# HGRN2 and pooling step on one Trainium2 core: transposing the decayed keys on VectorE and through memory instead of on TensorE

## Chip, cores and metric

One of the eight cores of a Trainium2 chip (trn2) runs the whole step. The metric is the device time of one execution in microseconds (us). TensorE is PE in the profile, VectorE is DVE, ScalarE is ACT, GpSimd is POOL, and SyncE, which issues every DMA of this kernel, is SP.

## What is computed

One inference step of a single layer: a gated linear recurrence (HGRN2) with four heads of 128 x 128 state, beside a pooling branch, both gated and merged. 2048 prompt tokens and 8 x 4 sample tokens pass the same weights. Cut to what the change touches:

```python
z = rmsnorm(x) @ w_in                       # split into q, f, i, g_a, u, g_b, m_a, m_b
fgate = lb + (1 - lb) * sigmoid(f)
logf, kin = log(fgate), 1 - fgate
# in chunks of 32 tokens, b = cumsum(logf) inside the chunk, ref = b at its middle
scores = (q * exp(b - ref)) @ (kin * exp(ref - b)).T        # masked to s <= t
o = scores @ v + (q * exp(b)) @ S
S = exp(b_last) * S + (kin * exp(b_last - b)).T @ v
o = rmsnorm(o) * silu(g_a)
out = x + (sigmoid(m_a) * (o @ w_proj_a) + sigmoid(m_b) * y_pool) @ w_out
```

All is float32. A large product is done as three products of values that are split into a high and a low part (`hi*hi + lo*hi + hi*lo`).

## The kernel before

The 2080 tokens go in five tiles of T = 416 tokens (features on the partitions, tokens along the free axis); the last tile has 384 prompt tokens and the 32 sample tokens. Each tile has NU = 56 slots, one for each block of weights, 128 x 1024. Slots 0 to 15 are the four heads, four slots each in the order f, q, i, g; then come the pooling inputs `u` and gates `b` (16 to 23), the merge gates and the two projections (24 to 47), and `out` (48 to 55). A slot is 24 matmuls of 128 x 416 on PE (`three`, L484 to L486).

Every engine has its program written out by slot, in one order that never changes; engines meet at semaphores. Weights flow so: SP loads block s + 2 into `wraw` in its slot s, after DVE has made the low part of block s (L401, L402). ACT in slot s copies block s + 3 into `whi` once PE has finished slot s - 1 (L763, L823), and DVE makes `wlo` of it at the start of its own slot s (`split`, L992). So SP is in its slot s when DVE is in slot s - 3, and both follow PE.

The recurrence of head h:

- slot 4h + 4: DVE makes the gate (`gated`, L1024), the state updates of head h - 1 (`updates`, L1110; in the last tile after the sums, with four of its eight sample states), the running sum of `logf` (`sums`, L1032 and L1042), `queries` (q2 and e1 at L1049 and L1051, four small copies of decays into `fac` at L1055, a scan into `dec`, the decayed queries `q4` at L1062). ACT makes the exponentials e3, e1, e2, e4 (`decays`, L797 to L805). POOL multiplies `e2` and `e4` by the keys (L1486, L1488).
- slot 4h + 5: DVE's `decayed_keys` (L1092) makes `qr0`, `qr1` and `kj4`, the keys decayed to the end of each 128-token block.
- slot 4h + 7: PE transposes `kj4` (L576, three of 128 x 128) and the last 32 columns of `e4` (L577) into bank B7, and computes the scores (L516 to L521). ACT copies the transposes to `ktm` (L837, L841). DVE copies the masked scores (`scores`, L1077 to L1082).
- slot 4h + 8: PE multiplies `ktm` with the values `vtm` (L539).
- slot 4h + 9: PE makes the outputs (`outputs`, L625, and L635, which waits for three state updates of DVE in its slot 4h + 8).

The values go another way. DVE transposes them in blocks of 32 x 32 (`values`, L1001 to L1003), and SP sends them out to `v_blocks` in memory with four DMAs, one for each 32 partitions, in pieces of 128 bytes (`values_out`, L455, slot 4h + 7), and back with two DMAs (`values_in`, L466 and L467, slot 4h + 9). That is where blocks change place.

The normed output of tile t - 1 is made by DVE in slots 5 to 8 of tile t, two of its eight parts in each slot (`output`, L1335), right after `split`. SP stores all 1,664 KB of it in slot 11 (`y_store`, L471), after the last part is made. Two more DMAs of that size are the loads of `xin` (L406) and `xres` (L433).

Of the kernel before, what the change touches and what calls it, by code (L numbers as in the profile page):

```python
# [114 lines left out]
def step_kernel(nc, xT, w_all, consts, w_pool, s_in, buf_in, yT, sp_out, pp_out, ss_out, ps_out):  # L115
    with ExitStack() as ctx:
# [57 lines left out]
        og = [buf["og0"], buf["og1"]]  # L174
        vt, logf, bc, dd, dl = buf["vt"], buf["logf"], buf["b"], buf["d"], buf["dl"]
# [91 lines left out]

        v_mem = nc.dram_tensor("v_blocks", (T, P), F32, kind="Internal").ap()
# [31 lines left out]
        kj_made, dq_made, ktm_made = sem("kj_made"), sem("dq_made"), sem("ktm_made")  # L300
# [6 lines left out]
        smasks, so_done, so_made, split_k, split_v = (sem("smasks"), sem("so_done"), sem("so_made"), sem("split_k"),  # L307
# [57 lines left out]

        def win_value(t, last, g, level, sample=False):
            before = sum(range(1, g + 1)) * (2 if last else 1)
            return t * 10 + before + (2 * level + sample if last else level) + 1
# [8 lines left out]
        def _(sp):  # L377
# [13 lines left out]
            def tile(t, last):  # L391
                for s in range(NU):
                    for h in range(H):
                        if s == 4 * h + 7:
                            values_out(t, h)
                        if s == 4 * h + 9:
                            values_in(t, last, h)
                    n = s + RAW
# [20 lines left out]
                    if last and s in (13, 17, 21, 25):  # L419
                        h = (s - 13) // 4  # L420
# [28 lines left out]
            def values_out(t, h):  # L449
# [30 lines left out]
        def _(pe):  # L480
# [7 lines left out]
            def small(t, last, s):  # L488
                for h in range(H):
# [5 lines left out]
                    if s == base + 7:  # L495
# [3 lines left out]
                        if not h:  # L499
                            pe.wait_ge(ybm_made, t * G)  # L500
                        elif last:
                            pe.wait_ge(s_made, s_value(t, last, h - 1, NG + 3))
                        else:
                            pe.wait_ge(ktm_made, nth(t, H, h - 1))
                        transposes(B7, kj4[:].rearrange("p g j n -> p (g j n)"), tk_done, e4)


# [17 lines left out]
                    if s == base + 8:  # L525


                        pe.wait_ge(ktm_made, nth(t, H, h))
# [24 lines left out]
                if s in MIX_SLOT:  # L553
# [4 lines left out]
                    if g == 1:  # L558
                        pe.wait_ge(ktm_made, nth(t, H, H - 1))
                    if g < 2:  # L560
# [3 lines left out]
                    three((B6, B7)[g % 2][:, 0:T], (wph[:, g, :], wplo[:, g, :]),  # L564
# [8 lines left out]

            def transposes(bank, src, done, rest):
                for g in range(NG):
                    pe.transpose(bank[:, g * P:(g + 1) * P], src[:, g * P:(g + 1) * P], ident[:])  # L576
                pe.transpose(bank[0:SAMPLE, 3 * P:4 * P], rest[:, PT:T], ident[:]).then_inc(done, 1)  # L577
# [181 lines left out]
        def _(act):  # L759
# [59 lines left out]
            def tile(t, last):  # L819
                for s in range(NU):  # L820
# [6 lines left out]
                    for h in range(H):  # L827
# [6 lines left out]
                        if s == 4 * h + 7:  # L834
                            act.wait_ge(tk_done, nth(t, H, h))
                            rest = B7[0:SAMPLE, 3 * P:4 * P]
                            act.activation(ktm[:, 0:3, :], B7[:, 0:3 * P].rearrange("p (g v) -> p g v", v=P), ACT.Copy)  # L837
                            if last:
                                high_rows(ks, rest, 1).then_inc(ktm_made, 1)
                            else:  # L840
                                act.activation(ktm[0:SAMPLE, 3, :], rest, ACT.Copy).then_inc(ktm_made, 1)  # L841
                        if s == 4 * h + 7 and last:
                            act.wait_ge(so_done, h + 1)
                            act.activation(so[h // 2][:], B6[:, 0:2 * P].rearrange("p (r v) -> p r v", v=P),
                                           ACT.Copy).then_inc(so_made, 1)
                            act.wait_ge(vtm_landed, 32 * nth(t, H, h))
# [141 lines left out]
        def _(dve):  # L988
# [56 lines left out]
            def queries(t, h):  # L1045

                dve.wait_ge(z_sem("q", h), z_done(t, "q", h))
                dve.wait_ge(exp_made, nth(t, 4 * H, 4 * h))
                dve.tensor_tensor(q2[h % 2][:], qf[h % 2][:], e3[h % 2][:], ALU.mult).then_inc(q_made, 1)  # L1049
                dve.wait_ge(exp_made, nth(t, 4 * H, 4 * h + 1))  # L1050
                dve.tensor_tensor(e1[:], qf[h % 2][:], e1[:], ALU.mult).then_inc(q_made, 1)  # L1051
# [10 lines left out]
                dve.tensor_tensor(q4[h % 2][:], q2[h % 2][:, 0:PT].rearrange("p (g j n) -> p g j n", g=NG, n=CHUNK),  # L1062
                                  dec[:, :, DQ:DQ + 4].unsqueeze(3).broadcast_to([P, NG, 4, CHUNK]),
                                  ALU.mult).then_inc(q_made, 1)

# [18 lines left out]

            def decayed_keys(t, h):

                dve.wait_ge(k_made, nth(t, 2 * H, 2 * h + 1))
                k2 = e4[:, 0:PT].rearrange("p (g j n) -> p g j n", g=NG, n=CHUNK)
                q = q2[h % 2][:, 0:PT].rearrange("p (g j n) -> p g j n", g=NG, n=CHUNK)

                def decayed(out, src, factors):
                    dve.tensor_tensor(out, src, factors.unsqueeze(len(src.shape) - 1).broadcast_to(list(src.shape)),  # L1092
                                      ALU.mult).then_inc(kj_made, 1)

                decayed(qr0[:], q[:, :, 1:4, :], dec[:, :, DR0:DR0 + 3])
                decayed(qr1[:], q[:, :, 2:4, :], dec[:, :, DR1:DR1 + 2])
                end = dec[:, :, DK + 3:DK - 1:-1]
                decayed(kj4[:, 0:NG:2], k2[:, 0:NG:2], end[:, 0:NG:2])
                decayed(kj4[:, 1, ::-1], k2[:, 1], end[:, 1])
# [18 lines left out]
            def updates(t, last, h):  # L1118
# [3 lines left out]
                if last:  # L1122
                    for b in range(4):
                        sample_update(t, h, b)
# [60 lines left out]
            def tile(t, last):  # L1185
                for s in range(NU):
# [16 lines left out]
                    if 5 <= s <= 8 and not first(t):  # L1203
                        output(t - 1, range(2 * s - 10, 2 * s - 8))
# [13 lines left out]
                    for h in range(H):  # L1218
# [6 lines left out]
                        if s == 4 * h + 4:  # L1225
                            gated(t, "g", h, ga[h % 3], sg_made, cst[:, C_GN:C_GN + 1])
                            if h and not last:
                                updates(t, last, h - 1)
                            sums(t, last, h)
                            if h and last:  # L1230
                                updates(t, last, h - 1)
                            queries(t, h)
                        if s == 4 * h + 5:
                            decayed_keys(t, h)
                        if s == 4 * h + 7:
                            scores(t, last, h)
                            if last:
                                dve.wait_ge(ktm_made, nth(t, H, h))
# [18 lines left out]
                        if s == 4 * h + 8 and h == H - 1:  # L1257
                            updates(t, last, h)
                        if s == 4 * h + 9 and last:
                            for b in range(4, NB):  # L1260
                                sample_update(t, h, b)
# [24 lines left out]
                    if s in MIX_SLOT:  # L1286
                        g = MIX_SLOT[s]
                        dve.wait_ge(mix_done, nth(t, G, g))
                        dve.wait_ge(z_sem("b", g), z_done(t, "b", g))
                        dve.tensor_tensor(bg[g % 3][:], (B6, B7)[g % 2][:, 0:T], bg[g % 3][:],  # L1290
                                          ALU.mult).then_inc(ybm_made, 1)
# [131 lines left out]
        def _(pool):  # L1423
# [54 lines left out]
            def tile(t, last):  # L1478
                for s in range(NU):
                    if s == 0 and not first(t):  # L1480
                        y_sum(t - 1, KD - 1)
                    for h in range(H):
                        if s == 4 * h + 4:
                            pool.wait_ge(kin_made, nth(t, H, h))
                            pool.wait_ge(exp_made, nth(t, 4 * H, 4 * h + 2))
                            pool.tensor_tensor(e2[:], kin[h % 2][:], e2[:], ALU.mult).then_inc(k_made, 1)  # L1486
                            pool.wait_ge(exp_made, nth(t, 4 * H, 4 * h + 3))
                            pool.tensor_tensor(e4[:], kin[h % 2][:], e4[:], ALU.mult).then_inc(k_made, 1)  # L1488
# [118 lines left out]
```

## Time and profile before

| | us |
|---|---|
| median of 3 runs | 1391.1 (1390.3 to 1391.17) |
| the profiled execution's own time | 1389.28 |
| its span, first to last instruction | 1387.6 |
| PE busy | 1372.1 (99%) |
| DVE busy | 921.9 (66%) |
| ACT busy | 687.5 (50%) |
| POOL busy | 241.6 (17%) |
| DMA, share of 16 engines | 42.5% |

The granted clock of TensorE was 0.997 of full speed. Busy PE is not PE at its peak: matmuls overlap, so that their recorded durations add up to more than the time they take, and the distance from start to start tells what one costs. The shares are means over stages: in the head slots DVE is at some 20 of 22 us.

### The profile page before, as it was taken

The numbers are of one execution on the slowest core, as the hardware profiler recorded it, in microseconds if no ns is written. First come the engines' busy times: TensorE is split into PE (matmuls) and PEld (weight loads), VectorE is DVE, ScalarE is ACT, GpSimd is POOL, SyncE is SP. The second block draws the span as 40 slices with busy tenths as digits, with TensorE's granted clock in tenths as the row PEclk, the third lists the DMA queues.
The fourth block names the chain that finished last, engine by engine and source line by source line (L and its number), as shares of the span: only waits on it lengthen the run. The fifth ranks groups of instructions, "written<-read, shape, count | busy, mean of one in ns | idle before, by whom it ended". The sixth has DMA issues, their size and how long they took to land.

```text
span 1387.6 us, 21227 instructions
## 1 busy us (share of the span) xinstructions
PE 1372.1 (99%) x8368; PEld 1358.0 (98%) x8368; DVE 921.9 (66%) x1538; ACT 687.5 (50%) x1016; POOL 241.6 (17%) x240
## 2 busy tenths in 40 slices
PE   9999999999999999999999999999999999999997
PEld 8999999999999999999999999999999999999997
DVE  7989655668874446688744567887445688974443
ACT  6565544355664343555633445565334455653332
POOL 2113121110131211111212110112220201130001
PEclk9999999999999999999999999999999999999998
DMA  6433533245335333453263334443533465534328
GB/s 201 126 109 113 204 123 118 95 128 185 107 107 205 122 121 107 123 171 121 96 219 108 121 108 137 154 127 107 205 120 97 133 165 172 159 112 170 111 103 96
DMA packets 97443, 187.52 MB, mean 135 GB/s; under 512 B 49088, under 2 KB 57664, under 8 KB 95680
## 3 DMA queue, kind: packets, MB, share of 16 engines
q1 hardware_dynamic: 97344, 186.16, 42.5%
q8 instruction: 67, 1.10, 0.3%
q14 instruction: 32, 0.26, 0.1%
HBM read 170.72 MB, written 15.42 MB: 134 GB/s over the span
## 4 chain that ended last, share of the span: by engine, by line
PE 93%; DVE 5%; ACT 1%; issue 1%; DVEq 0%; ACTq 0%
PE Z L484 29%; PE Z L486 28%; PE Z L485 28%; PE B L635 1%; DVE wlo L992 1%; PE B L539 1%; PE B L625 1%; DVE xres L1335 1%; PE B L516 1%; DVE h_b L1032 0%; PE B L576 0%; DVE fac L1055 0%; PE B L751 0%; ACT L857 0%; PE B L615 0%
## 5 line engine op out<-in xcount | busy, mean ns | idle before, releaser
L992 DVE TENSOR_TENSOR wlo<-wraw,whi 128x1024 fp32r<-128x1024 f32 x280 | 367.3, 1312 | 324.0 <-ACT whi L763 323.7
L484 PE MATMUL Z<-hhi,whi 128*128 128x416 f32 x1576 | 554.3, 352 | 0.0
L486 PE MATMUL Z<-hhi,wlo 128*128 128x416 f32 x1576 | 549.4, 349 | 0.0
L485 PE MATMUL Z<-hlo,whi 128*128 128x416 f32 x1576 | 549.4, 349 | 0.0
L763 ACT ACTIVATE whi<-wraw 128x1024 fp32r<-128x1024 f32 x280 | 295.3, 1056 | 424.6 <-PE Z L486 404.9
L484 PEld LDWEIGHTS Z<-hhi,whi 128*128 128x128 f32 x1576 | 296.0, 188 | 1.6 <-issue 0.8
L485 PEld LDWEIGHTS Z<-hlo,whi 128*128 128x128 f32 x1576 | 296.1, 188 | 0.4
L486 PEld LDWEIGHTS Z<-hhi,wlo 128*128 128x128 f32 x1576 | 295.9, 188 | 0.2
L486 PE MATMUL Z<-mhi,wlo 128*128 128x416 f32 x320 | 112.3, 351 | 0.0
L485 PE MATMUL Z<-mlo,whi 128*128 128x416 f32 x320 | 111.9, 350 | 0.0
L484 PE MATMUL Z<-mhi,whi 128*128 128x416 f32 x320 | 111.5, 348 | 0.0
L484 PE MATMUL Z<-yhi,whi 128*128 128x416 f32 x320 | 111.4, 348 | 0.0
L485 PE MATMUL Z<-ylo,whi 128*128 128x416 f32 x320 | 111.4, 348 | 0.0
L486 PE MATMUL Z<-yhi,wlo 128*128 128x416 f32 x320 | 111.4, 348 | 0.0
L1497 POOL TENSOR_TENSOR mA<-mA,mB 128x416 f32<-128x416 f32 x40 | 43.5, 1088 | 343.1 <-DVE mB L1171 343.1
L1486 POOL TENSOR_TENSOR h_e<-h_kin,h_e 128x416 f32<-128x416 f32 x20 | 25.1, 1255 | 373.0 <-ACT h_e L803 351.0
L1442 POOL TENSOR_TENSOR yacc<-yacc,ysq 128x416 f32<-128x416 f32 x34 | 37.0, 1089 | 158.4 <-ACT ysq L945 158.4
L1171 DVE TENSOR_TENSOR mB<-Z,gB 128x416 f32<-128x416 f32 x40 | 23.7, 592 | 58.6 <-PE Z L486 58.3
L1436 POOL TENSOR_TENSOR xacc<-xacc,xsq 128x416 f32<-128x416 f32 x28 | 41.9, 1495 | 114.0 <-ACT xsq L771 114.0
L485 PEld LDWEIGHTS Z<-mlo,whi 128*128 128x128 f32 x320 | 60.1, 188 | 0.6
L484 PEld LDWEIGHTS Z<-mhi,whi 128*128 128x128 f32 x320 | 60.1, 188 | 0.1
L486 PEld LDWEIGHTS Z<-yhi,wlo 128*128 128x128 f32 x320 | 60.1, 188 | 0.0
(240 smaller groups left out, 1667.6 us busy)
## 6 DMA issues: line engine op xcount, KB each, us to landing
wraw<-w_all SPq DMA_DIRECT2D x280, 512.0 KB, 3.5
xres<-xT SPq DMA_DIRECT2D x5, 1664.0 KB, 7.3
xin<-xT SPq DMA_DIRECT2D x4, 1664.0 KB, 8.0
yT<-xres SPq DMA_DIRECT2D x4, 1664.0 KB, 8.2
v_blocks<-h_vt SPq DMA_DIRECT2D x80, 52.0 KB, 2.5
vtm<-v_blocks SPq DMA_DIRECT2D x20, 192.0 KB, 3.4
s<-s_in SPq DMA_DIRECT2D x4, 512.0 KB, 5.8
ss_out<-snew SPq DMA_DIRECT2D x4, 512.0 KB, 5.4
```

The source lines that it names most:

```text
L484: pe.matmul(out, wh, xh, start=first, stop=False)
L485: pe.matmul(out, wh, xl, start=False, stop=False)
L486: return pe.matmul(out, wl, xh, start=False, stop=final)
L516: pe.matmul(B4[rows(g, j), at + CHUNK:(g + 1) * P], e4[:, at:at + CHUNK], after[j], start=True, stop=True)
L539: mm = pe.matmul(B6[:, g * P:(g + 1) * P], ktm[:, g, :], vtm[:, g, :], start=True, stop=True)
L763: act.activation(whi[n % RING][:], raw(t, n)[:], ACT.Copy).then_inc(whi_made, 1)
L992: dve.tensor_tensor(wlo[n % RING][:], raw(t, n)[:], whi[n % RING][:].bitcast(F32), ALU.subtract).then_inc(wlo_made, 1)
L1171: dve.tensor_tensor(out[j % 2][:], z_bank(acc, j)[:, 0:T], gate[j % 3][:], ALU.mult).then_inc(z_sem(acc, j), 1)
L1436: pool.tensor_tensor(xacc[:], xacc[:], xsq[k % 2][:], ALU.add).then_inc(xacc_made, 1)
L1442: pool.tensor_tensor(yacc[:], yacc[:], ysq[j % 2][:], ALU.add).then_inc(yacc_made, 1)
L1486: pool.tensor_tensor(e2[:], kin[h % 2][:], e2[:], ALU.mult).then_inc(k_made, 1)
L1497: pool.tensor_tensor(mA[j % 2][:], mA[j % 2][:], mB[j % 2][:], ALU.add).then_inc(merged, 1)
```

## The change

It makes `ktm`, the keys with tokens on the partitions, in the way in which the values are made.

- DVE transposes `kj4`, and in tiles 0 to 3 the last 32 columns of `e4`, in blocks of 32 x 32 into `kt` (new, it shares its place with `logf`). SP sends `kt` to `k_blocks` in memory (`keys_out`, four DMAs) and, when that has landed, back into `ktm` (`keys_in`, two DMAs, in the last tile one). Both stand in SP's slot 4h + 8, with `values_in` between them, which was in slot 4h + 9.
- PE's transposes go, except the one of the sample keys in the last tile; ACT's copies into `ktm` go too. PE waits in slot 4h + 8 for `ktm_landed`.
- The two key products move from POOL to DVE. On DVE the decay copies and the scan (`decay_factors`) stand ahead of the query products, then comes `keys` (e4, `kj4`, transposes), then `decayed_queries` (e2, `q4`, `qr0`, `qr1`), all in slot 4h + 4.
- In the last tile the updates of head h - 1 stand ahead of the sums, and the sample states move to slots 4h + 9 and 4h + 10 (their stores on SP one slot later).
- DVE's `output` moves from behind `split` to the end of slots 5 to 8. The product of pooling and gate moves from the end of a slot to its start, and the pooling banks B6 and B7 change places.
- ACT's `Ln` into `logf` waits for the keys of the head before to be in memory.

```diff
@@ sync
-                        if s == 4 * h + 9:
+                        if s == 4 * h + 8:
+                            keys_out(t, last, h)
                             values_in(t, last, h)
+                            keys_in(t, last, h)
...
+            def keys_out(t, last, h):
+                n = t * H + h
+                rows_out = PT if last else T
+                sp.wait_ge(kt_made, n + 1)
+                if n:
+                    sp.wait_ge(ktm_landed, k_value(t, last, h - 1) if h else 32 * n)
+                for a in range(4):
+                    sp.dma_start(k_mem[0:rows_out, a * CHUNK:(a + 1) * CHUNK].rearrange("(c i) j -> i c j", i=CHUNK),
+                                 kt[a * CHUNK:(a + 1) * CHUNK, 0:rows_out].rearrange("p (c j) -> p c j", j=CHUNK)
+                                 ).then_inc(k_kept, 16)
+            def keys_in(t, last, h):
+                n = t * H + h
+                sp.wait_ge(k_kept, n * 64 + 64)
+                sp.wait_ge(p_done, t * H + h * (3 if last else 1))
+                sp.dma_start(ktm[:, 0:NG, :], k_mem[0:PT].rearrange("(g p) v -> p g v", p=P)).then_inc(ktm_landed, 16)
+                if not last:
+                    sp.dma_start(ktm[0:SAMPLE, 3, :], k_mem[PT:T]).then_inc(ktm_landed, 16)
@@ tensor
-                        transposes(B7, kj4[:].rearrange("p g j n -> p (g j n)"), tk_done, e4)
+                        if last:
...
+                            pe.transpose(B7[0:SAMPLE, 3 * P:4 * P], e4[:, PT:T], ident[:]).then_inc(tk_done, 1)
...
-                        pe.wait_ge(ktm_made, nth(t, H, h))
+                        pe.wait_ge(ktm_landed, k_value(t, last, h))
@@ scalar
+                act.wait_ge(k_kept, 64 * (t * H + h))
                 act.activation(logf[:], sf[h % 2][:], ACT.Ln, bias=lb0[:, h:h + 1],
...
-                            act.activation(ktm[:, 0:3, :], B7[:, 0:3 * P].rearrange("p (g v) -> p g v", v=P), ACT.Copy)
@@ vector
+            def keys(t, last, h):
+                dve.wait_ge(kin_made, nth(t, H, h))
+                dve.wait_ge(exp_made, nth(t, 4 * H, 4 * h + 3))
+                dve.tensor_tensor(e4[:], kin[h % 2][:], e4[:], ALU.mult).then_inc(k_made, 1)
...
+                decayed(kj4[:, 0:NG:2], k2[:, 0:NG:2], end[:, 0:NG:2])
+                decayed(kj4[:, 1, ::-1], k2[:, 1], end[:, 1])
+                dve.wait_ge(k_kept, 64 * (t * H + h))
+                dve.wait_ge(kj_made, nth(t, KJ * H, KJ * h + 1))
+                ins = dve.transpose(kt[:, 0:PT], kj4[:].rearrange("p g j n -> p (g j n)"))
+                if not last:
+                    ins = dve.transpose(kt[:, PT:T], e4[:, PT:T])
+                ins.then_inc(kt_made, 1)
...
-                    if 5 <= s <= 8 and not first(t):
-                        output(t - 1, range(2 * s - 10, 2 * s - 8))
...
-                            if h and not last:
+                            if h:
                                 updates(t, last, h - 1)
                             sums(t, last, h)
-                            if h and last:
-                                updates(t, last, h - 1)
+                            decay_factors(t, h)
                             queries(t, h)
-                        if s == 4 * h + 5:
-                            decayed_keys(t, h)
+                            keys(t, last, h)
+                            decayed_queries(t, h)
...
+                    if 5 <= s <= 8 and not first(t):
+                        output(t - 1, range(2 * s - 10, 2 * s - 8))
@@ gpsimd
-                            pool.tensor_tensor(e2[:], kin[h % 2][:], e2[:], ALU.mult).then_inc(k_made, 1)
...
-                            pool.tensor_tensor(e4[:], kin[h % 2][:], e4[:], ALU.mult).then_inc(k_made, 1)
```

Two places show how it moves instructions. The first is DVE in tile 1, slot 8, which is slot 4h + 4 of head 1: here before, from its `split` (L992) on, with `xres` the two `output` steps.

```order
L992 TENSOR_TENSOR wlo_58<-wraw_50,whi_54 128x1024
L1335 SCALAR_TENSOR_TENSOR xres<-xres,cst,yrs 128x416 x2
L1024 SCALAR_TENSOR_TENSOR h_ga_119<-Z,cst,h_ga_119 128x416
L1110 SCALAR_TENSOR_TENSOR s_all<-carry,dec,B 128x128
...
L1032 SCALAR_TENSOR_TENSOR h_b<-smask,h_logf 128x416
...
L1049 TENSOR_TENSOR h_q_117<-h_qf_129,h_e_115 128x416
L1051 TENSOR_TENSOR h_e_111<-h_qf_129,h_e_111 128x416
L1055 COPY fac<-h_e_115 128x3x4
...
L1062 TENSOR_TENSOR q_1_194<-h_q_117,dec 128x384
L992 TENSOR_TENSOR wlo_55<-wraw_49,whi_51 128x1024
```

And the same slot of the change:

```order
L1014 TENSOR_TENSOR wlo_58<-wraw_50,whi_54 128x1024
L1046 SCALAR_TENSOR_TENSOR h_ga_119<-Z,cst,h_ga_119 128x416
...
L1054 SCALAR_TENSOR_TENSOR h_b<-smask,h_logf 128x416
...
L1072 COPY fac<-h_e_115 128x3x4
...
L1089 TENSOR_TENSOR h_e_113<-h_kin_131,h_e_113 128x416
L1105 TENSOR_TENSOR kj_193<-h_e_113,dec 128x2x128
L1105 TENSOR_TENSOR kj_193<-h_e_113,dec 128x4x32
L1098 STREAM_TRANSPOSE kt<-kj_193 128x384
L1100 STREAM_TRANSPOSE kt<-h_e_113 128x32
L1110 TENSOR_TENSOR h_e_112<-h_kin_131,h_e_112 128x416
...
L1375 SCALAR_TENSOR_TENSOR xres<-xres,cst,yrs 128x416 x2
L1014 TENSOR_TENSOR wlo_55<-wraw_49,whi_51 128x1024
```

The output steps were the second row and are now the last ones of the slot, behind the keys and the transposes.

The second place is SP in tile 1, slots 11 and 12: before,

```order
L455 DMA v_blocks<-h_vt 32x13x32 x4
L402 DMA wraw_50<-w_all 128x1024
L471 DMA yT<-xres 128x3328
L402 DMA wraw_49<-w_all 128x1024
L466 DMA vtm<-v_blocks 128x3x128
L467 DMA vtm<-v_blocks 32x128
```

and now:

```order
L465 DMA v_blocks<-h_vt 32x13x32 x4
L412 DMA wraw_50<-w_all 128x1024
L502 DMA yT<-xres 128x3328
L477 DMA k_blocks<-kt 32x13x32 x4
L497 DMA vtm<-v_blocks 128x3x128
L498 DMA vtm<-v_blocks 32x128
L486 DMA ktm<-k_blocks 128x3x128
L488 DMA ktm<-k_blocks 32x128
L412 DMA wraw_49<-w_all 128x1024
```

The keys of head 1 stand behind the store `yT` of the previous tile's output, and the weights of slot 14 (the last row) behind the keys.

## Rows read from the trace of the kernel before

**Rows 1.** The page's chain that ended last, by engine.

```profile
PE 93%; DVE 5%; ACT 1%; issue 1%; DVEq 0%; ACTq 0%
```

**Rows 2.** Waits of PE: total us, times, longest.

```profile
PE B L635 <- DVE carry L1110: 2.4, 3, 1.5
```

**Rows 3.** Timeline of PE, tile 1: start us, duration, engine, line, out<-in.

```profile
336.95 0.49 PE L576 MATMUL B<-ident,kj 128*128 128x128 f32 x3
...
337.48 0.27 PE L516 MATMUL B<-qr,h_e 128*32 128x96 f32 x2
...
343.15 0.60 PE L539 MATMUL B<-vtm,ktm 128*128 128x128 f32 x4
...
349.33 0.47 PE L635 MATMUL B<-q,s_all 128*128 128x128 f32 x2
```

**Rows 4.** Timeline of DVE, tile 1, head 0, slots 4 and 5.

```profile
304.91 1.02 DVE L1032 TENSOR_TENSOR_SCAN h_b<-smask,h_logf 128x416 f32<-128x416 f32 x1 [0.67 <-ACT h_logf L797]
...
306.99 0.58 DVE L1049 TENSOR_TENSOR h_q<-h_qf,h_e 128x416 f32<-128x416 f32 x1
...
307.99 2.11 DVE L1055 COPY fac<-h_e 128x12 f32<-128x12 f32 x4
...
310.89 1.22 DVE L992 TENSOR_TENSOR wlo<-wraw,whi 128x1024 fp32r<-128x1024 f32 x1
312.02 1.21 DVE L1335 SCALAR_TENSOR_TENSOR xres<-xres,cst,yrs 128x416 f32<-128x416 f32 x2
313.15 0.72 DVE L1092 TENSOR_TENSOR qr<-h_q,dec 128x288 f32<-128x288 f32 x2
313.79 0.62 DVE L1092 TENSOR_TENSOR kj<-h_e,dec 128x256 f32<-128x256 f32 x2
```

**Rows 5.** Groups by line and shape: DVE's block transpose; busy us, mean ns.

```profile
L1001 DVE STREAM_TRANSPOSE h_vt<-Z 128x256 f32<-128x256 f32 x20 | 8.8, 438 | 0.1
```

**Rows 6.** Timeline of POOL, tile 1, head 0: the first key product.

```profile
307.74 1.29 POOL L1486 TENSOR_TENSOR h_e<-h_kin,h_e 128x416 f32<-128x416 f32 x1 [16.97 <-ACT h_e L803]
```

**Rows 7.** Timeline of DVE, last tile, head 1: the decay copies.

```profile
1147.41 0.38 DVE L1055 COPY fac<-h_e 128x12 f32<-128x12 f32 x4
```

**Rows 8.** DMA issues on the page: count, KB each, median us to landing.

```profile
wraw<-w_all SPq DMA_DIRECT2D x280, 512.0 KB, 3.5
xres<-xT SPq DMA_DIRECT2D x5, 1664.0 KB, 7.3
...
v_blocks<-h_vt SPq DMA_DIRECT2D x80, 52.0 KB, 2.5
vtm<-v_blocks SPq DMA_DIRECT2D x20, 192.0 KB, 3.4
```

**Rows 9.** Timeline of DVE, tile 1, slots 7 and 8: scores, updates, sums.

```profile
319.75 0.22 DVE L1077 COPY s_all<-carry 128x128 f32<-128x128 f32 x1
...
324.93 0.34 DVE L1110 SCALAR_TENSOR_TENSOR s_all<-carry,dec,B 128x128 f32<-128x128 f32 x1
...
326.34 1.02 DVE L1032 TENSOR_TENSOR_SCAN h_b<-smask,h_logf 128x416 f32<-128x416 f32 x1
```

**Rows 10.** Timeline of SP, tile 1: the store of tile 0's output.

```profile
324.48 0.36 SPq L471 DMA_DIRECT2D yT<-xres  x1
```

**Rows 11.** SP at tile 0's end, and the weights issued from 154.2 to 156.

```profile
152.93 0.33 SPq L406 DMA_DIRECT2D xin<-xT  x1
155.27 0.33 SPq L402 DMA_DIRECT2D wraw<-w_all  x1
...
wraw<-w_all SPq DMA_DIRECT2D x1, 512.0 KB, 6.3
```

**Rows 12.** PE's start; then a stretch past its end (busy, count, PEclk, DMA, GB/s).

```profile
2.73 5.49 PE L751 MATMUL B<-at_sb,ones_r 128*128 128x384 f32 x8 [2.73 <-DVE ones_r L1344]
...
1380.00:1381.00 1.00, 0.00 (x0) 0.00 (x0) 0.99 (x2) 0.00 (x0) 0.00 (x0) 0.74 0.00 0
1381.00:1382.00 1.00, 0.00 (x0) 0.00 (x0) 1.00 (x3) 0.00 (x0) 0.00 (x0) 0.50 0.00 0
```

More of the change, by code:

```diff
@@ L266, in step_kernel @@
         B4, B5, B6, B7 = [ctx.enter_context(nc.psum_tensor(f"B{i}", [P, 512], F32)) for i in range(4, 8)]
+        k_mem = nc.dram_tensor("k_blocks", (T, P), F32, kind="Internal").ap()
         v_mem = nc.dram_tensor("v_blocks", (T, P), F32, kind="Internal").ap()
@@ L364, in p_value, with k_value @@
             return t * H + h * (3 if last else 1) + i + 1
+        def k_value(t, last, h):
+            return 32 * t * H + (16 if last else 32) * (h + 1)
         def win_value(t, last, g, level, sample=False):
@@ L418, in tile @@
                         sp.dma_start(exts[:, :, :, 0:BUF], buf_in).then_inc(buf_landed, 16)
-                    if last and s in (13, 17, 21, 25):
-                        h = (s - 13) // 4
+                    if last and s in (14, 18, 22, 26):
+                        h = (s - 14) // 4
                         sp.wait_ge(s_made, s_value(t, last, h, NG + NB - 1))
@@ L557, in small @@
                     pe.wait_ge(pml_made, nth(t, G, g))
-                    if g == 1:
-                        pe.wait_ge(ktm_made, nth(t, H, H - 1))
-                    if g < 2:
+                    if g == 0 and last:
+                        pe.wait_ge(s_made, s_value(t, last, H - 1, NG + 3))
+                    elif g == 0:
+                        pe.wait_ge(ybm_made, t * G)
+                    elif g == 1:
                         pe.wait_ge(s_made, s_value(t, last, H - 1, NG + NB - 1 if last else 3))
@@ L572, in small @@
                     y_squares(t - 1, False)
[L574 to L577, printed above, removed]
             def sample_products(h, bank, v):
@@ L833, in tile @@
                             sigmoid(t, "g", h, ga[h % 3], sg_made)
-                        if s == 4 * h + 7:
-                            act.wait_ge(tk_done, nth(t, H, h))
-                            rest = B7[0:SAMPLE, 3 * P:4 * P]
-                            act.activation(ktm[:, 0:3, :], B7[:, 0:3 * P].rearrange("p (g v) -> p g v", v=P), ACT.Copy)
[L838 to L841, printed above, removed]
                         if s == 4 * h + 7 and last:
+                            act.wait_ge(tk_done, h + 1)
+                            high_rows(ks, B7[0:SAMPLE, 3 * P:4 * P], 1).then_inc(kh_made, 1)
                             act.wait_ge(so_done, h + 1)
@@ L845, in tile @@
                                            ACT.Copy).then_inc(so_made, 1)
+                        if s == 4 * h + 7 and last:
                             act.wait_ge(vtm_landed, 32 * nth(t, H, h))
@@ L1061, in queries, with decayed, decayed_queries @@
+            def decayed(out, src, factors):
+                dve.tensor_tensor(out, src, factors.unsqueeze(len(src.shape) - 1).broadcast_to(list(src.shape)),
+                                  ALU.mult).then_inc(kj_made, 1)
+            def decayed_queries(t, h):
+                dve.tensor_tensor(e2[:], kin[h % 2][:], e2[:], ALU.mult).then_inc(k_made, 1)
                 dve.wait_ge(q_made, nth(t, 3 * H, 3 * h))
-                dve.tensor_tensor(q4[h % 2][:], q2[h % 2][:, 0:PT].rearrange("p (g j n) -> p g j n", g=NG, n=CHUNK),
-                                  dec[:, :, DQ:DQ + 4].unsqueeze(3).broadcast_to([P, NG, 4, CHUNK]),
+                q = q2[h % 2][:, 0:PT].rearrange("p (g j n) -> p g j n", g=NG, n=CHUNK)
+                dve.tensor_tensor(q4[h % 2][:], q, dec[:, :, DQ:DQ + 4].unsqueeze(3).broadcast_to([P, NG, 4, CHUNK]),
@@ L1064, in queries @@
                                   ALU.mult).then_inc(q_made, 1)
+                decayed(qr0[:], q[:, :, 1:4, :], dec[:, :, DR0:DR0 + 3])
+                decayed(qr1[:], q[:, :, 2:4, :], dec[:, :, DR1:DR1 + 2])
             def chunk_decay(h):
@@ L1083, in scores @@
                                     B4[0:SAMPLE, PT:T]).then_inc(b4_read, 1)
[L1085 to L1099, printed above, removed]
             def update(t, last, h, g):
@@ L1121, in updates, with sample_updates @@
                     update(t, last, h, g)
-                if last:
-                    for b in range(4):
-                        sample_update(t, h, b)
+            def sample_updates(t, h, at):
+                for b in range(at, at + 4):
+                    sample_update(t, h, b)
             def sample_update(t, h, b):
@@ L1226, in tile @@
                             gated(t, "g", h, ga[h % 3], sg_made, cst[:, C_GN:C_GN + 1])
-                            if h and not last:
+                            if h:
                                 updates(t, last, h - 1)
                             sums(t, last, h)
-                            if h and last:
-                                updates(t, last, h - 1)
+                            decay_factors(t, h)
                             queries(t, h)
-                        if s == 4 * h + 5:
-                            decayed_keys(t, h)
+                            keys(t, last, h)
+                            decayed_queries(t, h)
+                        if s == 4 * h + 8 and h == H - 1:
+                            updates(t, last, h)
+                        if s == 4 * h + 9 and last:
+                            sample_updates(t, h, 0)
                         if s == 4 * h + 7:
@@ L1256, in tile @@
                                         ALU.mult).then_inc(vms_made, 1)
[L1257 to L1261, printed above, removed]
+                        if s == 4 * h + 10 and last:
+                            sample_updates(t, h, 4)
                         if s == 4 * h + 13:
```

50 lines of the change are left out of this document (26 added, 24 removed).

## The prediction, made before the change was run

> **What bounds the kernel now.** I read the chain of waits first: 93% of it is TensorE (PE) [rows 1]. Then the waits of PE: after the start it hardly waits; the largest item is 2.4 us in three waits for the state updates of VectorE (DVE) at L635, the longest 1.5 [rows 2]. So the time is PE's own instruction stream, and the change can do two things: shorten that stream, or make PE wait where it does not wait now. The timelines of tile 1 then give the distances between the engines, the DMA page and the queue of SyncE (SP) the price of a trip through memory.
>
> **What leaves PE.** The three transposes of decayed keys and the one of sample keys start at 336.95; the next instruction of PE starts at 337.48 [rows 3]: 0.53 us per head. The change removes all four in tiles 0 to 3 (16 heads, 8.5 us) and three of four in the last tile (4 heads, 0.33 us each, 1.3 us). That is 9.8 us of a stream that hardly waits, and the whole of what can be gained there. The copies of `ktm` that ScalarE (ACT) made lay in idle time and are worth nothing.
>
> **What DVE gets and loses.** Added per head: the two key products, 0.50 us each like the two query products that fill 306.99 to 307.99 [rows 4], and the block transposes of 384 and 32 columns. No row shows them; the nearest takes 0.438 us for 256 columns from PSUM [rows 5]: 0.66 plus about 0.1, so 0.75 us (between 0.44 and 0.9). Sum 1.75 us. Removed: nothing in the list, but the four tiny copies into `fac` fill 307.99 to 310.1 while GpSimd (POOL) runs the key products from 307.74 [rows 4, 6]; in the last tile, for a head whose copies start after POOL is done, the same four take 0.38 us [rows 7]. With POOL's products gone I take 0.42 us each time: 1.7 us back. The cause is inferred; if it is another one, DVE is 1.7 us later per head (a rival below). The Trainium skill, in "SBUF — State Buffer", on the shared port pair, says that VectorE copies in a two-port mode and GpSimd instructions lock each other out for a whole instruction. By that rule the copies take their short time; the trace agrees.
>
> **The new path of the keys, tile 1.** Head 0: scan at 304.91, sums 2.08 us to 306.99 [rows 4]; then copies 0.42, decay scan 0.28, two query products 1.0, key product 0.5, decayed keys 0.54, transposes 0.75: `kt` is ready at 310.5. Four DMAs out take 2.0 us of SP's issue, the last starting 1.5 after the first and landing 2.5 later [rows 8]: 314.5. Keys in: second DMA issued at 314.95, 3.4 to land [rows 8]: 318.4. PE wants them about 320, so head 0 does not wait. The weights of slot 10 are issued behind that on SP, at 315.4, where they were issued at about 312.1; 3.5 to land, 1.06 on ACT, 1.13 for the split on DVE: 321.1. Mask copies and value transposes 1.4 us (from 319.75, [rows 9]), two outputs 1.13, the next split 1.13, the gate 0.56, updates 1.41: these end at 326.8, the third at 326.45, where PE arrives at 326.5. Just in time.
>
> **The store of the previous tile's output is the trouble.** In slots 5 to 8 DVE's two `output` steps move from the slot's start to its end. SP's slot 11 waits for the last two, and SP's slot 12 holds `keys_out` of head 1. Before, the store was issued at 324.48 [rows 10], and nothing that was urgent stood behind it. Now head 1 goes: updates end 326.8, sums 328.9, the same steps to `kt` at 332.4, key product of `e2`, decayed queries and `qr` 1.6 (334.0), outputs 1.13: the store is issued at 335.1, and only then can SP issue keys that were ready 2.7 us earlier. 1,664 KB take 7.3 us by the like transfer `xres` [rows 8]: landed at 342.4. Do the keys overtake it? Weights issued at 155.27, behind `xin` of 152.93, took 6.3 us and not 3.5 [rows 8, 11]: they landed at 161.6, 1.4 after the big one could land. So no. Behind it come 1,664 pieces of 128 bytes; taking for them their own landing time of 2.5, the keys are in memory at 344.9. The Trainium skill, in "DMA: Bandwidth & Descriptors", section on queues, rings and completion order, says that on each DMA engine descriptors of one queue are consumed in ring order: the trace agrees with it.
>
> Keys back: second DMA issued 345.4, landed 348.8. PE's products of head 1 started at 343.15 [rows 3]; less two heads' transposes, PE is ready at 342.1. **It waits 6.7 us.** Then the weights of slot 14: SP was held until 345.8, so they land at 349.3, reach DVE's split by 351.5; mask and values 1.4, split 1.13, gate 0.5, three updates 1.1: 355.75. PE, from 348.8 plus the 6.2 us between its L539 and L635 [rows 3], is there at 355.0 and waits 0.75. Against 349.33 before, 6.4 us late. Heads 2 and 3 save 0.53 each, since there the loop of `kt`, trip through memory, weights, split, updates, sums and next `kt` adds up to 21.0 us against PE's 21.8: 5.4 us lost per tile in tiles 1 to 3.
>
> **Clock.** TensorE's granted clock was 1.00 (2.4 GHz) while PE worked, 0.74 in the second us after its last instruction, which ended at 1379, and 0.50 (1.2 GHz) in the third [rows 12]. An idle stretch of 6.7 us therefore ends at 1.2 GHz. At the start of the program PE ran its first four products at about 1.37 us each, from 2.73 to 8.2 [rows 12], and at full pace after. 5.5 us at half pace lose 2.7; the 0.75 us wait behind is swallowed: 2.0 us per tile (bounds 0 and 3.5). The Trainium skill, "TensorE: Matmul & The Clock Gate", Part 1, has the same two levels and says that idling leads to the lower one; the trace agrees.
>
> **Sum.** Tile 0 has no store: 4 x 0.53 saved, 2.1 (DVE is nearly full there; bounds 0 and 3). Tiles 1 to 3: 3 x 7.4 = 22.2. Last tile: PE's pace per head is slower and DVE has 1.9 us more between split and value transposes, while its waits at L635 (2.4 us [rows 2]) go, since updates now stand ahead of the sums; I take plus 4.5 (2 to 8). -2.1 + 22.2 + 4.5 = +24.6 us. The profiled execution took 1389.3, 0.13% below the median of 1391.1; against it 1413.9, so **1414 us, slower by 1.7%**.
>
> **Rivals.**
> 1. *Faster: keys don't queue behind the store.* If pieces of both share the DMA engines, the keys of head 1 are in memory at 339.2 and back at 343.1, 1 us after PE is ready. It decides at 342.1: landed sooner, nothing is left but the 9.8 us less about 5 of small waits (the head-1 updates, tile by tile). 1384 us. Against it: the 6.3 us of the weights behind `xin`. 10%.
> 2. *DVE's copies stay slow.* 1.7 us later per head: loop 22.7 against 21.8, so 0.8 more for 20 heads, and 1.7 more in each of four idle stretches: 1414 + 16 + 7 = 1437. For it: the cause is inferred from three heads of the last tile. 8%.
> 3. *Idle stretches as worked out, but no clock loss:* 1414 - 7 = 1407. 20%.
> 4. *The store's tail is shorter:* keys land with it (1 to 2 us less in each tile): 1407 to 1410. Inside the forecast.
>
> Forecast 60% (1407 to 1424); 2% for a loss of under 0.2%. Range of 8 in 10: from 1398 (rival 3 with each tile's wait 2 us shorter) to 1430. Faster or slower by under 0.2% can't be told from no change here. Faster 0.10, same 0.03, slower 0.87.
>
> **What would show it.** Right: in each of tiles 1 to 4 one wait of PE of 5 to 8 us at L568 on the landing of `ktm` from `k_blocks`, none of that size in tile 0; `yT` issued some 10 us later in the tile than before, with k_blocks landing 7 us or more after issue; `fac` copies at 0.15 us; a granted clock below 1 after the wait. Wrong: PE waits in every head alike (rival 2, or the loop through memory), or no wait over 2 us (rival 1). Store ahead of the keys but no wait of PE would break the whole argument.

## The result, and the profile after

Median 1439.33 us (1435.14 to 1440.66 in 4 runs) against 1390.7: a ratio of 1.0345 [1.0323, 1.0368], slower by about 3.5%. The forecast was 1414, its range ended at 1430. The direction was right, the size was half.

The profiled execution took 1435.14 us, 4 below that median; its span is 1433.0, against 1387.6. The chain that ended last, by engine, which was 93% PE [rows 1]:

```profile
PE 72%; DVE 12%; DMA 7%; issue 3%; ACT 3%; SPq 3%; DVEq 0%; ACTq 0%
```

Waits of PE (us in total, times, longest), where before nothing was over 2.4 us in total after the start [rows 2]:

```profile
PE B L641 <- DVE at_sb L1134: 29.9, 8, 9.3
PE B L619 <- DVE snew L1174: 4.7, 3, 2.3
PE B L661 <- DVE s_all L1146: 4.1, 4, 2.1
PE B L641 <- DVE ats L1134: 3.4, 1, 3.4
```

L641 is the first product of `sum_squares`; in slot 4h + 12 it sums the squares of head h's output into bank B4. L568, the product with `ktm` at which the forecast put its wait, is not in the list (one wait of 0.2). L1134 is the last of DVE's masked copies of the scores, which empties B4. In the kernel before the same wait was one of 0.3 us:

```profile
PE B L615 <- DVE at_sb L1082: 0.3, 1, 0.3
```

The keys' DMAs on the page. `wraw` (3.5) and `xres` (7.3) are as in [rows 8], `v_blocks` took 2.7 for 2.5, and the store `yT` 5.7 where the page of before had 8.2:

```profile
yT<-xres SPq DMA_DIRECT2D x4, 1664.0 KB, 5.7
...
vtm<-v_blocks SPq DMA_DIRECT2D x20, 192.0 KB, 2.5
ktm<-k_blocks SPq DMA_DIRECT2D x20, 192.0 KB, 2.3
k_blocks<-kt SPq DMA_DIRECT2D x64, 52.0 KB, 1.9
```

Tile 1, slot 12, from the timeline (start us, duration, engine, line; in brackets the idle time before and what ended it):

```profile
339.20 0.36 SPq L502 DMA_DIRECT2D yT<-xres  x1
339.65 4.27 SPq L477 DMA_DIRECT2D k_blocks<-kt  x4
...
346.38 0.38 SPq L486 DMA_DIRECT2D ktm<-k_blocks  x1
...
347.33 7.48 SPq L412 DMA_DIRECT2D wraw<-w_all  x3
352.14 1.06 ACT L789 ACTIVATE whi<-wraw 128x1024 fp32r<-128x1024 f32 x1 [13.35 <-DMA wraw<-w_all]
353.23 1.23 DVE L1014 TENSOR_TENSOR wlo<-wraw,whi 128x1024 fp32r<-128x1024 f32 x1 [9.97 <-ACT whi L789]
...
354.98 0.17 DVE L1134 COPY_PREDICATED at_sb<-cmask,B 32x32 f32<-32x32 uint32 x1
...
355.29 0.68 PE L641 MATMUL B<-sqh,ones_r 128*128 128x416 f32 x1 [9.29 <-DVE at_sb L1134]
...
356.12 1.48 PE L568 MATMUL B<-vtm,ktm 128*128 128x128 f32 x6
```

Read from the bottom. PE stands 9.29 us at the squares. It waits for mask copies that stand on DVE behind the split of block 14 (L1014); the load of block 14 is the first of the three `wraw` loads from 347.33, which SP issues behind `keys_in`; `keys_in` waits until the keys are in memory; and the keys stand behind the store. So the store, the keys and the weights are in the order that was forecast, but the wait ends 6 us later than the arrival of `ktm` (346.8 plus 2.3), because it hangs on the weights, one link further. L568 comes right behind, with `ktm` long there.

How far the head products (L568, before L539) start behind those of before, head 3 of each tile: 3.1 us in tile 0, then 13.9, 25.6, 36.2, and 45.3 in the last tile. So tile 0 lost 3.1, tiles 1 to 3 10.9, 11.6 and 10.6, the last tile 9.2. Tile 0 varies: three of the experiments below run the same instructions there (the outputs back, the store two slots later, the filler) and lost 5.0, 5.1 and 4.7 in it.

### The profile page after: what moved, and what is told of

Same layout as the page of the kernel before. It is cut to its first block, busy times and chain, and to the rows that moved or that the text cites. A ratio compares the mean times of both kernels' runs of the same rounds, so it can differ in the third digit from the quotient of the medians.

```text
span 1433.0 us, 21246 instructions
## 1 busy us (share of the span) xinstructions
PE 1376.6 (96%) x8292; PEld 1357.2 (95%) x8292; DVE 916.1 (64%) x1614; ACT 679.4 (47%) x980; POOL 194.4 (14%) x200
## 4 chain that ended last, share of the span: by engine, by line
PE 72%; DVE 12%; DMA 7%; issue 3%; ACT 3%; SPq 3%; DVEq 0%; ACTq 0%
PE Z L515 23%; PE Z L517 22%; PE Z L516 22%; DMA wraw<-w_all 4%; DMA k_blocks<-kt 3%; ACT whi L789 2%; SPq L477 2%; DVE wlo L1014 1%; DVE h_b L1054 1%; DVE xres L1375 1%; DVE kj L1105 1%; DVE h_d L1064 1%; DVE s_all L1146 1%; DVE h_e L1089 1%; DVE h_dl L1064 1%
## 5 line engine op out<-in xcount | busy, mean ns | idle before, releaser
L1014 DVE TENSOR_TENSOR wlo<-wraw,whi 128x1024 fp32r<-128x1024 f32 x280 | 366.0, 1308 | 373.2 <-ACT whi L789 372.9
L1508 POOL TENSOR_TENSOR pa<-ext 128x430 f32<-128x430 f32 (+1 forms) x20 | 26.9, 1343 | 587.0 <-ACT ext L898 361.3
L515 PEld LDWEIGHTS Z<-yhi,whi 128*128 128x128 f32 x320 | 60.1, 188 | 0.0
L516 PEld LDWEIGHTS Z<-ylo,whi 128*128 128x128 f32 x320 | 60.1, 188 | 0.0
```

The source lines that it names most:

```text
L515: pe.matmul(out, wh, xh, start=first, stop=False)
L516: pe.matmul(out, wh, xl, start=False, stop=False)
L1014: dve.tensor_tensor(wlo[n % RING][:], raw(t, n)[:], whi[n % RING][:].bitcast(F32), ALU.subtract).then_inc(wlo_made, 1)
L1508: pool.tensor_tensor(wins(level)(first, BUF + n), a, b, ALU.add).then_inc(win_made, 1)
```

## Experiments

Each kernel is the change with one edit, unless it says otherwise; "before" ran beside each.

**The store's place.** DVE's `output` steps go back behind the split, and so the store goes out some 6 us earlier (at 333.04 in tile 1):

```diff
@@ vector, tile, behind the y_split of slot YNORM - 2
+                    if 5 <= s <= 8 and not first(t):
+                        output(t - 1, range(2 * s - 10, 2 * s - 8))
@@ the same function, end of the slot
-                    if 5 <= s <= 8 and not first(t):
-                        output(t - 1, range(2 * s - 10, 2 * s - 8))
```

> The change with DVE's two output steps put back right behind the split in slots 5 to 8; all else as changed. Theory A (the late store holds SP and the DMA rings in front of the keys and of the weights of slot 14, and that sets PE's long wait at L641): the store is issued ahead of the keys being ready, the four waits of 3.4 to 9.3 us and their low clock go, and what is left is tile 0's loss (3 us by the start of tile 1) in each tile or less: 1396 us, between 1388 and 1404. Theory B (the loop keys, memory, weights, split, updates is too long in every head, whatever the store does): at most a third of the loss goes, 1420 us or more.

1413.99 us, ratio 1.0177 [1.0160, 1.0194]. Putting the store back gave 25 us, but theory A had it take nearly the whole loss away: 24 us stayed where it said 6. The result lies between the ranges of the two theories, so neither holds as it stands. PE's waits here:

```profile
PE B L641 <- DVE at_sb L1134: 9.4, 8, 3.8
PE B L661 <- DVE s_all L1146: 8.2, 4, 2.5
```

Every tile still loses some: 5.0, 5.4, 4.6, 3.4 and 4.6 us. In tile 1, with no store near, a `wraw` load is still issued only behind `keys_in`, and ACT and DVE wait for it (timeline):

```profile
319.75 0.48 SPq L488 DMA_DIRECT2D ktm<-k_blocks  x1
320.28 8.13 SPq L412 DMA_DIRECT2D wraw<-w_all  x3
...
326.82 1.22 DVE L1014 TENSOR_TENSOR wlo<-wraw,whi 128x1024 fp32r<-128x1024 f32 x1 [3.81 <-ACT whi L789]
```

The hold of weights behind keys is a second cause, and it acts in tile 0 too.

**Weights ahead of `keys_in`.**

```diff
@@ sync, tile, slot 4h + 8
-                            keys_in(t, last, h)
...
                         sp.dma_start(wraw[n % RAW][:], w_all[n % NU]).then_inc(w_landed[n % RAW], 16)
+                    for h in range(H):
+                        if s == 4 * h + 8:
+                            keys_in(t, last, h)
```

> The change with SP's reads of ktm (and their wait for the keys to be in memory) moved behind the weight load of the same slot, so that this load (block 4h + 10) no longer waits for the keys to land. Theory A: in the head with the store it starts only 2 us earlier, since the wait for the store and the keys' pieces stay ahead of it: 4 x 2 us; in tile 0 the wait of 2.1 us at L661 and its low clock go, 3 to 5 us: 1427 us, between 1420 and 1433. Theory B: the loop gets some 3 us shorter in every head, and nearly all of the loss goes: under 1405 us.

1420.17 us, 1.0218 [1.0203, 1.0234]: 19 us less than the change, where 12 were expected; the at_sb waits fell from 29.9 to 20.7.

**The store two slots later on SP** (`if s == 13` for `if s == 11`), behind the keys of head 1.

> The change with SP's store of the previous tile's output in slot 13 (behind the keys of head 1 and the weights of slots 14 and 15) instead of slot 11; DVE's order as changed. Theory A: the keys go out when they are ready, and the long waits go as in e1: 1396 us, 1388 to 1406. Theory B, or a cause on DVE (the late output steps as such): 1430 us or more.

1413.38 us, 1.0171 [1.0156, 1.0186], above the range of 1388 to 1406. The same as with the outputs back: it is the order on SP that costs 25 us, wherever it is mended.

**The outputs late, but in the kernel before**, with nothing else of the change.

> The kernel before with only one part of the change: DVE's output steps at the end of slots 5 to 8, so the store is issued some 10 us later, with no keys behind it. Theory A: the late store costs nothing where no urgent transfer stands behind it on SP: 1391 us, within 0.3%. Rival (the store's 1,664 KB collide with the weights there in any case): 1400 us or more.

1391.59 us, 1.0011 [1.0002, 1.0020]. The late store alone costs 1.7 us; to cost more, it needs something urgent behind it.

**Both first edits together.**

> Both edits of e1 and e2: output steps back behind the split, and SP's weight load ahead of the reads of ktm. Two causes (the late store; weights of block 4h + 10 held behind the keys on SP), each of which was found worth 25 and 19 us alone. If they are separate, the sum goes: 1439 - 44 = 1395 us, between 1390 and 1401. If they are one cause seen twice (whatever shortens SP's hold helps once), it stays at 1410 or more. Faster than before (1390) only if also the waits that the shorter DVE path leaves are under 9.8 us of PE.

1397.4 us, 1.0050 [1.0035, 1.0065]. 25 and 19 us alone, 42 together: two causes that nearly add.

**Keys issued by GpSimd.** `keys_out` and `keys_in` unchanged but on POOL's own queue, at the start of its slot 4h + 4; store and outputs late as in the change.

```diff
@@ sync, slot 4h + 8
-                            keys_out(t, last, h)
                             values_in(t, last, h)
-                            keys_in(t, last, h)
@@ gpsimd
+                    for h in range(H):
+                        if s == 4 * h + 4:
+                            keys_out(t, last, h)
+                            keys_in(t, last, h)
```

> The change with keys_out and keys_in issued by POOL (idle in these slots) instead of SP; store and outputs late as changed. If SP's order is the cause, SP now waits for none of the keys: weights come when they did before, the keys don't wait for the store: 1395 us, 1385 to 1405, with POOL's own time to issue them as the unknown. If the time of the trip through memory itself is the cause (keys late at PE), it stays over 1415 and PE waits for ktm at L568 or the like.

1418.0 us, 1.0197 [1.0181, 1.0212]: over the 1415 of the alternative, but not for its reason, since PE waits for `ktm` only 0.3 us in tile 1. The keys never stand behind the store, yet PE waits up to 4.2 us for `at_sb`. The DMAs issued between 330 and 350 us (median us to landing):

```profile
yT<-xres SPq DMA_DIRECT2D x1, 1664.0 KB, 7.2
wraw<-w_all SPq DMA_DIRECT2D x3, 512.0 KB, 7.5
k_blocks<-kt POOLq DMA_DIRECT2D x4, 52.0 KB, 2.1
...
ktm<-k_blocks POOLq DMA_DIRECT2D x1, 192.0 KB, 6.7
```

The weights now stand directly behind the late store, and take 7.5 us for 3.5; `ktm`, from another queue, takes 6.7 beside it, where the median of its 20 loads in this run is 3.6. So what is in flight with the store is slowed, from either queue; the share of the weights in the 6.7 was not separated.

**The same with the outputs back.**

> e7 with the output steps back behind the split. If SP's order is the whole cause: no wait over 2 us on PE, near the 9.8 us that the change takes off PE: 1383 us, between 1379 and 1392. If DVE's path from the sums to kt, or POOL's slow issue, still makes PE wait: 1392 to 1405.

1395.39 us, 1.0033 [1.0021, 1.0046]. About the time of both edits on SP, as its second case had it. Its products lost 4.9 us in tile 0 (3.6 of it one wait for the first `ktm`), and nothing more in tiles 1 to 3, though each had a wait of about 1 us for `at_sb`.

**Does the clock cost anything?** PE is kept busy through the wait with 40 products into an idle bank:

```diff
@@ tensor, small, slot 12, ahead of the wait for b4_read
+                        if h == 0 and not first(t) and not last:
+                            pe.wait_ge(ybm_made, t * G)
+                            for _ in range(40):
+                                pe.matmul(B7[:, 0:T], ones_r[:], hhi[0][:], start=True, stop=True)
```

> The change with 40 matmuls of 128x416 into bank B7, which nothing reads, on PE just ahead of the wait in slot 12 of tiles 1 to 3: they take 7.5 us inside a wait of 9. They leave all waits as they are and keep TensorE's clock at 2.4 GHz. If the low clock after the wait costs what I had put on it (2 us a tile, bounds 0 and 3.5): 6 us less, 1433 us, between 1428 and 1437, with a granted clock of 1.00 behind the wait in tiles 1 to 3. If it costs nothing because DVE's chain is what PE meets next: no change, 1439 us.

1434.47 us, 1.0321 [1.0305, 1.0336]: 4.9 us less than the change, 1.6 for each of three tiles. The two intervals overlap, so this difference alone isn't clear of noise; the two traces are plainer. From the start of the squares in slot 12 to the start of the 24th weight product behind them, the same instructions take 7.00, 7.18 and 7.75 us in tiles 1, 2 and 3 of the change, and 5.64, 5.65 and 5.65 with the filler: 1.4, 1.5 and 2.1, or 5.0 us together. Not all of it was kept: tiles 1 to 3 lost 33.1 us in the profiled execution of the change and 30.5 with the filler. Stretches of tile 1 (busy time and count of PE, PEld, DVE, ACT, POOL; then the granted clock, the DMA share and GB/s), first of the change:

```profile
347.00:350.00 3.00, 0.00 (x0) 0.00 (x0) 0.00 (x0) 0.00 (x0) 0.00 (x0) 0.65 0.68 163
350.00:353.00 3.00, 0.00 (x0) 0.00 (x0) 0.00 (x0) 0.86 (x1) 0.00 (x0) 0.50 0.68 264
...
355.00:357.00 2.00, 1.71 (x7) 1.71 (x8) 2.00 (x7) 1.87 (x2) 0.00 (x0) 0.50 0.74 231
357.00:359.00 2.00, 2.00 (x11) 1.98 (x11) 1.33 (x4) 0.00 (x0) 0.00 (x0) 0.71 0.83 146
```

and with the filler:

```profile
355.00:357.00 2.00, 0.66 (x5) 0.61 (x5) 2.00 (x8) 1.98 (x3) 0.00 (x0) 1.00 0.36 41
357.00:359.00 2.00, 2.00 (x16) 2.00 (x15) 1.96 (x4) 0.99 (x2) 0.00 (x0) 1.00 0.74 255
```

The clock stays at 2.4 GHz instead of falling to 1.2. (The counts of products in single rows can't be compared, since PE stands at different instructions in them.)

**Is bank B4 the link?** DVE's mask copies of slot 4h + 7 ahead of that slot's split, and nothing else:

```diff
@@ vector, tile
+                    for h in range(H):
+                        if s == 4 * h + 7:
+                            scores(t, last, h)
                     if (s + AHEAD < NU or not last) and not (first(t) and s + AHEAD < FIRST):
                         split(t, s + AHEAD)
...
                         if s == 4 * h + 7:
-                            scores(t, last, h)
```

> The change, with the mask copies of VectorE in slot 4h + 7 ahead of that slot's split, so that bank B4 is read without waiting for weights. Theory (the 9.3 us wait is the mask copies standing behind the split of late weights): the waits of PE for at_sb are gone (under 1 us each in tiles 1 to 3); what is next is the landing of ktm, which is issued at 346.4 in tile 1 of the change and lands about 349, 3 to 4 us after PE comes, and then the state updates behind the same late split, about 2.5 us. Per tile 5 to 6 us of waits in place of 9.3: 1425 us (1418 to 1431). Rival (the mask copies only stand in for it: what holds PE is the late weights in any case): 1439, with as long a wait at the updates or at the weights.

1413.24 us, 1.0168 [1.0153, 1.0184]: 26 us less, nearly twice what was expected, and under its range. Tile 1:

```profile
334.25 0.36 SPq L502 DMA_DIRECT2D yT<-xres  x1
...
341.51 0.38 SPq L486 DMA_DIRECT2D ktm<-k_blocks  x1
...
344.22 1.44 PE L568 MATMUL B<-vtm,ktm 128*128 128x128 f32 x6 [2.70 <-DMA ktm<-k_blocks]
...
352.83 0.94 PE L661 MATMUL B<-q,s_all 128*128 128x128 f32 x6 [0.55 <-DVE s_all L1146]
```

This is the picture that the forecast drew: a wait for `ktm` at L568, then a short one at L661. The `ktm` wait is 2.70 us, not 6.7. Tile 0 gains 1.3 us, and tiles 1 to 3 lose 5.1, 5.3 and 4.4 where the forecast had 7.4. The last tile loses 10.6, now with 5.9 us of PE waiting at L568 for ACT's `so`, the states of the sample tokens. On ACT that copy stands behind the one into `whi`, which waits for weights that SP issued behind `keys_in` (last tile):

```profile
1175.68 0.38 SPq L486 DMA_DIRECT2D ktm<-k_blocks  x1
1176.11 7.08 SPq L412 DMA_DIRECT2D wraw<-w_all  x3
...
1180.52 1.06 ACT L789 ACTIVATE whi<-wraw 128x1024 fp32r<-128x1024 f32 x1 [12.30 <-DMA wraw<-w_all]
...
1182.03 0.38 ACT L865 ACTIVATE so<-B 128x256 f32<-128x256 f32 x1
```

So the late weights reach PE there by yet another link.

**The mask copies first, in the better versions.** With outputs back and weights first:

> Outputs back behind the split, weights ahead of keys_in, and the mask copies ahead of the split. The version before it (1397.4) had 5.6 us of waits for at_sb in 7 pieces; the theory gives back 3 to 4 us of them, since the state updates come next: 1394 us (1390 to 1397). Rival: no gain, 1397.

1387.82 us, 0.9985 [0.9976, 0.9994], better than its range. With the keys on GpSimd and outputs back:

> Keys issued by GpSimd, outputs back behind the split, and the mask copies ahead of the split. The version without the last edit (1395.4) had 4.7 us of waits for at_sb in 5 pieces: 1392 us (1389 to 1395). Rival: no gain, 1395.

1389.79 us, 0.9997 [0.9988, 1.0005]. And with the keys of tile 0 on SP, weights between, those of later tiles on GpSimd:

> As the last one, but in tile 0 SyncE sends and fetches the keys, with the weights between. With GpSimd tile 0 lost 4.9 us against before, 3.6 of it one wait for the first ktm; with SyncE, weights first, it lost 0.7. Later tiles lost nothing more with GpSimd. So 1388 us (1385 to 1391), which would be the first version under before (1390). Rival: the loss of tile 0 is not the issue by GpSimd, 1392.

1386.43 us, 0.9982 [0.9973, 0.9991]. PE's waits here, after the start:

```profile
PE B L634 <- DVE snew L1189: 4.7, 3, 2.1
...
PE B L583 <- DMA ktm<-k_blocks: 1.9, 1, 1.9
PE B L623 <- DVE vms L1317: 0.6, 1, 0.6
```

From tile 1 to tile 3 there is no wait in the head slots at all, and against before each head gains another 0.26 to 0.45 us, 0.35 in the mean: the transposes, gained at last, though less than the 0.53 that they seemed to take. At head 0 of the last tile the lead is 5.5 us; three waits for sample states at L634, all in the last tile, give some of it back, and 3.5 us of the span are left. The medians of the first and the last of these three differ by 1.4 us and their intervals overlap, so neither is shown to be the faster; both lie some 0.2% under before.

## Why the prediction was too small

The sum was made for tile 0, tiles 1 to 3 and the last tile: -2.1, three times 7.4, +4.5. Measured on the profiled execution: +3.1, +10.9, +11.6, +10.6, +9.2. (The 24.6 us were added to the profiled execution's 1389.3 and called a median; on the median of 1391.1 they give 1415.7. That changes nothing.)

**The step that failed: "Just in time", and the search for PE's next deadline behind it.** The forecast followed the late weights of slot 4h + 10 into DVE's split and then only to the updates (L661). It let the mask copies run in that chain (1.4 us with the value transposes), but never asked what waits for them on PE. They empty bank B4, and PE needs that bank for the squares of the head before, in slot 4h + 8 of the head whose scores are copied, ahead of the products. With the forecast's own numbers (weights of slot 14 landed at 349.3, the splits of DVE to 351.5, then about 0.8 for the mask copies) PE, ready at 342.1, would have waited until 352.3, 10.2 us; it waited 9.3. Taking only that link away (mask copies first) gave back 26 us, as much as the store's place does. The second failed term is the last tile: it was put at 4.5 with no row for what it loses, and lost 9.2.

- *Tile 0, forecast -2.1.* It lost 3.1 (4.7 to 5.1 in three other runs of the same instructions), since the weights wait for the trip of the keys there too: with the weights first it lost 1.0. With the mask copies first it gained 1.3. A wait at L661 was written down only for the store's tiles: here PE waited 2.1 us at it.
- *Tiles 1 to 3, forecast 7.4.* The mechanism (store, then keys, then weights in one queue) was right: removed at either end, 25 us go. The store was issued at 339.20; less tile 0's drift of 3.1 that is 336.1 against 335.1. The tail was shorter than worked out: keys in memory by 346.4, 7.2 after the store's issue and not 9.8, and `ktm` back in 2.3 and not 3.4. The store had landed at 344.9, so the keys came 1.5 behind it and not 2.5, and the store itself took 5.7 and not 7.3. This is near rival 4, but it makes the time shorter, and is too small to make up for the missed link.
- *Clock, forecast 2.0 per tile.* 1.4, 1.5 and 2.1 by the filler's traces; in time, 1.6 a tile at most is seen. So rival 3 (no loss) is out. What was missed is that the clock falls in tile 0 as well (below).
- *Last tile, forecast 4.5, bounds 2 to 8.* 9.2. The 2.4 us of waits at L635 did go, but 4.7 us at L619 came, 1.3 at L608, and 3.4 at L641 for `ats`, the sample part of the same mask copies.
- *What left PE, 0.53 per head.* Too much: 0.35 per head in the mean of tiles 1 to 3 of the last version, or some 7 us in all for the 9.8 (an estimate, 20 heads at 0.35).
- *DVE's costs.* Right. The copies into `fac` take 0.15 to 0.17 us in all 80 cases (the maximum before was 1.07), and four of them 0.39 us together, the 0.42 taken [rows 4, 7]; rival 2 is out. The Trainium skill, "SBUF — State Buffer", on the shared port pair, has VectorE copies in a two-port mode and GpSimd instructions lock each other out; by that rule the copies get short when POOL's products go, and the trace agrees. The transpose of 384 columns took 0.58 us, where 0.66 was taken [rows 5]:

```profile
L1072 DVE COPY fac<-h_e x80: 153/161/172, 35.9 to 1237.0; 128x12 f32<-128x12 f32 x20, 128x6 f32<-128x6 f32 x20, 128x3 f32<-128x3 f32 x20, 128x9 f32<-128x9 f32 x20
```

```profile
L1098 DVE STREAM_TRANSPOSE kt<-kj 128x384 f32<-128x384 f32 x20 | 11.6, 579 | 2.5 <-DVE kj L1105 0.5
```

- *Rival 1 (faster, the keys don't queue).* Out: the store had landed at 344.9 (339.20 plus 5.7), the keys only then, by 346.4. And where they really didn't stand behind it, issued by GpSimd, the kernel was slower by 2% all the same, because the weights stood there instead: with the store early again it took 22.6 us less.

Three kernels came out at 1413 to 1414 us, the number of the forecast. In the one with the mask copies first, that is near its mechanism, but with smaller tiles and a larger last tile; the agreement of the sums is chance.

## What to carry to other kernels

When an instruction is made late, list every semaphore that stands behind it on its engine, bank releases too, and find the first place at which the waited-for engine meets any of them; the wait that you looked for may never come up. A load that a queue holds behind a trip through memory is as late as that trip: issue the weights between the way out and the way in. And a late transfer is only as harmful as what is issued behind it: the same move cost 1.7 us in the old kernel and 25 in the new.

## What the runs showed of the hardware

A wait of 2.1 us can be followed by a lower clock, and need not be. In tile 0 of the change PE waited 2.13 us up to 56.11, behind a wait of 0.30 up to 52.90, and then worked without a pause (same columns as above):

```profile
54.00:56.00 2.00, 0.00 (x0) 0.00 (x0) 1.93 (x5) 1.94 (x2) 0.00 (x0) 1.00 1.06 271
56.00:58.00 2.00, 1.89 (x13) 1.86 (x14) 1.93 (x5) 0.55 (x1) 0.00 (x0) 0.95 0.85 252
58.00:60.00 2.00, 2.00 (x8) 1.92 (x7) 1.97 (x10) 1.96 (x4) 0.00 (x0) 0.50 0.06 23
60.00:62.00 2.00, 2.00 (x9) 1.96 (x8) 1.79 (x6) 1.98 (x4) 0.00 (x0) 0.70 0.00 0
```

The fall to 1.2 GHz came when PE was busy again, from about 58 to 61. In the kernel before the clock stayed at 1.00 from 54 to 66. The last version (1386.43 us) has a wait of 2.13 us as well, up to 1176.0 in its last tile, and there the clock stayed at 1.00:

```profile
1173.00:1176.00 3.00, 0.87 (x47) 0.69 (x45) 2.97 (x8) 1.54 (x4) 0.00 (x0) 1.00 0.44 116
1176.00:1179.00 3.00, 3.00 (x29) 2.79 (x30) 2.90 (x8) 0.88 (x3) 0.00 (x0) 1.00 0.23 93
```

What made the difference no run here shows. The other surprise is on SP: four DMAs of 128-byte pieces took 4.27 us to issue behind the store (339.65), where they took 1.88 with nothing before them in tile 0.
